# Where the modulation blocks stand: layer 1's move from the MLP product into layer 0's q, k, v and gelu products

## The reference

```python
for l in range(DEPTH):                                   # DEPTH = 2
    mod = (silu(c) @ ada_w[l] + ada_b[l])[:, None, :]    # ada_w[l]: 1024 x 6144
    sh1, sc1, g1, sh2, sc2, g2 = split(mod, 6)
    modc = silu(c_ctx) @ ada_w[l] + ada_b[l]
    h = modulate(rms_norm(x, mix_pre_g[l]), sh1, sc1)    # modulate: h * (1 + scale) + shift
    p = h @ w_in[l]                                      # q, k, v, gelu u, gelu v, conv, gates
    ...
    x = x + g1 * rms_norm(y, mix_post_g[l])
    h2 = modulate(rms_norm(x, ffn_pre_g[l]), sh2, sc2)
    x = x + g2 * rms_norm(square(relu(h2 @ w_ff1[l])) @ w_ff2[l], ffn_post_g[l])
    # the context xc goes the same way with modc, in layer 0
```

## Time and profile before

| | |
|---|---|
| median of 3 runs | 4638.47 us (4631.3 to 4643.43) |
| profiled execution | 4643.45 us, its span 4641.7 us |
| PE busy | 4279.6 us, 92% of the span |
| DVE, ACT, POOL busy | 1254.8, 723.8, 388.0 us |
| mean granted clock of TensorE | 0.954 of full speed |
| chain that ended last | PE 90%, DVE 4%, ACT 4% |

### The profile page before, as it was taken

One profiled execution on the slowest core, in us unless ns is written; L12 is line 12 of the kernel. 1 busy time (PEld: TensorE's weight loads), 2 busy tenths in 40 slices (PEclk: granted clock), 3 DMA queues, 4 the chain that ended last, 5 costly groups with the idle time before them and its releaser, 6 DMA issues.

```text
span 4641.7 us, 34590 instructions
## 1 busy us (share of the span) xinstructions
PE 4279.6 (92%) x13429; PEld 2226.9 (48%) x13429; DVE 1254.8 (27%) x2499; ACT 723.8 (16%) x1393; POOL 388.0 (8%) x250
## 2 busy tenths in 40 slices
PE   7998899997989999997999998989997878699999
PEld 3454555554535445443454443434443467454444
DVE  1213407981010000012341693010003054531010
ACT  2104300002020000002151001110001231231000
POOL 1100002540200000000000132100000001000000
PEclk8999999998999999999999999999998987599999
DMA  5310011111111232221201221222212100101221
GB/s 206 136 55 18 5 55 38 53 55 36 37 68 68 91 127 73 74 72 57 73 19 41 73 73 55 86 84 75 73 68 75 47 19 0 46 29 63 73 78 67
DMA packets 137133, 294.21 MB, mean 63 GB/s; under 512 B 5050, under 2 KB 13290, under 8 KB 137008
## 3 DMA queue, kind: packets, MB, share of 16 engines
q1 hardware_dynamic: 120096, 236.58, 14.5%
q0 software_dynamic: 16912, 55.83, 3.6%
HBM read 290.22 MB, written 2.18 MB: 63 GB/s over the span
## 4 chain that ended last, share of the span: by engine, by line
PE 90%; DVE 4%; ACT 4%; DMA 1%; issue 1%; POOL 0%; DVEq 0%; ACTq 0%; SPq 0%
PE psum L1629 45%; PE psum L1685 14%; PE psum L1891 12%; PE psum L926 5%; PE psum L1623 3%; PE psum L1731 2%; ACT sb_rc L1401 1%; PE psum L1714 1%; PE psum L1671 1%; ACT sb_ht L1401 1%; PE psum L724 1%; DMA sb_ring<-in_ada_w 1%; PE psum L737 1%; PE psum L738 1%; PE psum L1850 0%
## 5 line engine op out<-in xcount | busy, mean ns | idle before, releaser
L1629 PE MATMUL psum<-sb_ht,sb_ring 128*128 128x512 f32 (+1 forms) x4496 | 1664.0, 532 | 16.9 <-ACT sb_rc L1401 8.1
L1629 PEld LDWEIGHTS psum<-sb_ht,sb_ring 128*128 128x128 f32 x4496 | 853.6, 190 | 823.7 <-issue 789.9
L1891 PE MATMUL psum<-sb_ring,sb_rc 128*128 128x512 f32 x1280 | 553.6, 593 | 7.6 <-DVE sb_rc L2142 7.6
L2011 DVE SCALAR_TENSOR_TENSOR sb_rc<-sb_rc,sb_vec x960 | 475.7, 575 | 0.1
L1685 PE MATMUL psum<-sb_ring,sb_ht 128*128 128x512 f32 (+1 forms) x1088 | 458.0, 582 | 2.8 <-ACT sb_ht L1401 2.8
L1891 PEld LDWEIGHTS psum<-sb_ring,sb_rc 128*128 128x128 f32 x1280 | 241.9, 190 | 318.6 <-issue 308.6
L1401 ACT ACTIVATE sb_rc<-psum 128x512 f32 (+3 forms) x238 | 124.9, 545 | 1346.9 <-PE psum L1629 1109.5
L1685 PEld LDWEIGHTS psum<-sb_ring,sb_ht 128*128 128x128 f32 x1088 | 205.9, 190 | 253.3 <-issue 246.8
L1629 PE MATMUL psum<-sb_rc,sb_ring 128*128 128x512 f32 (+1 forms) x768 | 282.0, 529 | 27.6 <-ACT sb_rc L1401 27.6
L1401 ACT ACTIVATE sb_kvt<-psum 128x512 f32<-128x512 f32 (+2 forms) x209 | 105.7, 533 | 1073.1 <-PE psum L1629 852.8
L1623 PE MATMUL psum<-sb_ident,sb_rb 128*128 128x128 f32 (+2 forms) x836 | 135.7, 306 | 142.4 <-DVE sb_rb L1915 37.2
(11 more groups left out here) (288 smaller groups left out, 2741.1 us busy)
## 6 DMA issues: line engine op xcount, KB each, us to landing
sb_ring<-in_w_in SPq DMA_DIRECT2D x37, 2048.0 KB, 7.9
sb_ring<-in_w_ff SPq DMA_DIRECT2D x32, 2048.0 KB, 8.4
sb_ring<-in_w_ffn SPq DMA_DIRECT2D x16, 2048.0 KB, 8.2
sb_kvt<-in_ada_w POOLq DMA_DIRECT2D x12, 2048.0 KB, 9.1
sb_rc<-in_ada_w POOLq DMA_DIRECT2D x8, 2048.0 KB, 8.2
sb_ring<-in_w_out SPq DMA_DIRECT2D x6, 2048.0 KB, 7.8
sb_ring<-in_ada_w SPq DMA_DIRECT2D x4, 2048.0 KB, 12.5
sb_ring<-in_w_gmlp_o SPq DMA_DIRECT2D x4, 2048.0 KB, 7.8
```

Of the source, the lines that this page charges most:

```text
L1629: last = pe.matmul(bank(b + v, m), ring[:, slot, k, j * P:(j + 1) * P], rhs[:, k, a:a + m], start=k == 0, stop=k == KT - 1)
L1891: last = pe.matmul(bank(i), hid[:, KT * kb + k, i * P:(i + 1) * P], ring[:, slot, k, :], start=kb == 0 and k == 0, stop=kb == 1 and k == K ...
L2011: step = stt(conv_slot(j, a, m), conv_slot(j + 1, a + k, m), vec[:, j, k:k + 1], conv_slot(j, a, m), op0=ALU.mult, op1=ALU.add)
```

## The change

All twenty late blocks now stand between groups of layer 0's q, k, v products and gelu u products. Blocks 0 to 11 come after groups 1, 2, 4, 5, 7, 8, 10, 11, 13, 14, 16 and 17 of q, k, v; blocks 12 to 19 after the eight groups of gelu u. The second MLP product has none. All use one weight buffer in `rc`, with the small rows behind it. From block 11 on the results go to banks 6 and 7, before to 0 and 1. Layer 1's blocks' rows are made by DVE inside `normalise_heads`. ACT waits for the last store ahead of the gelu v results, since these overwrite the buffer.

```diff
-        LATE0, LATE = 8, 20
+        LATE0, LATE_B, LATE = 12, 11, 20
...
-        QKV_LATE = [2, 4, 6, 8, 10, 12, 14, 16]
-        order = [(f, c, kb, i) for f in range(2) for c in range(2) for kb in range(2) for i in range(AT)]
-        FF_LATE, FF_LAST = order[2:2 + 3 * (LATE - LATE0):3], order[2 + 3 * (LATE - LATE0)]
+        QKV_LATE = [1, 2, 4, 5, 7, 8, 10, 11, 13, 14, 16, 17]
...
-            if n < LATE0:
-                w, rows, flat = rc[:, RD:RD + KT * COLS], rc, RD - 4 * COLS
-            else:
-                w, rows, flat = kvt[:, 0:KT * COLS], rb, 3 * DM
-            piece = [rows[:, flat + i * COLS:flat + (i + 1) * COLS] for i in range(4)]
+            w = rc[:, RD:RD + KT * COLS]
+            piece = [rc[:, RD + (KT + i) * COLS:RD + (KT + i + 1) * COLS] for i in range(4)]
...
 # PE, late_part(k)
+                if k == LATE_B:
+                    pe.wait_ge(*s_qkv_sb.at(0, 16))
...
 # PE, after the q, k, v products
                 if l == 0:
-                    late_sum(LATE0 - 1)
-                channel_major(s_gu_ps, l, s_gu_sb, 2, 0, ht, l, [s_late_row.at(0, LATE0)] if l == 0 else ())
+                    pe.wait_ge(*s_late_st.at(0, LATE_B))
+                    pe.wait_ge(*s_late_row.at(0, LATE_B))
+                channel_major(s_gu_ps, l, s_gu_sb, 2, 0, ht, l, (),
+                              after=(lambda j: late(LATE0 + j)) if l == 0 else None)
+                if l == 0:
+                    late_sum(LATE - 1)
                 for c in range(2):
-                    token_major(s_gv_ps, l, s_gv_sb, c * n, n, ht, [s_qkv_sb.at(l, 2 * n + AT)] if c == 0 else ())
+                    before = [s_qkv_sb.at(l, 2 * n + AT)] + ([s_late_row.at(0, LATE)] if l == 0 else [])
+                    token_major(s_gv_ps, l, s_gv_sb, c * n, n, ht, () if c else before)
...
 # PE, second MLP product
-                                if l == 0 and (f, c, kb, i) in FF_LATE:
-                                    late(LATE0 + FF_LATE.index((f, c, kb, i)))
-                                if l == 0 and (f, c, kb, i) == FF_LAST:
-                                    late(LATE)
...
 # DVE, normalise_heads, tile u
                     ch.meet()
+                    if l == 0 and u % 2:
+                        late_row(LATE0 - 1 + u // 2)
...
 # ACT, after the q, k, v results
+                drain(s_gu_ps, l, s_gu_sb, lambda j, v, a, m: u_cm[:, j, a:a + m], 0, ACT.Gelu_apprx_tanh,
+                      (lambda j: late_stage(LATE0 + j)) if l == 0 else None)
                 if l == 0:
-                    act.wait_ge(*s_late_out.at(0, 16 * LATE0))
-                drain(s_gu_ps, l, s_gu_sb, lambda j, v, a, m: u_cm[:, j, a:a + m], 0, ACT.Gelu_apprx_tanh)
+                    act.wait_ge(*s_late_out.at(0, 16 * LATE))
```

More of the change, by code:

```diff
@@ L1315, in late_columns @@
             def late_columns(l, parts):
-                pool.wait_ge(*s_late_out.at(0, 16 * (LATE if l else LATE0)))
+                pool.wait_ge(*s_late_out.at(0, 16 * LATE))
                 for part in parts:
@@ L1337, in _ @@
                     late_load(0)
-                    for k in range(1, LATE0):
+                    for k in range(1, LATE):
                         late_load(k)
                         late_store(k - 1)
-                    late_store(LATE0 - 1)
+                    late_store(LATE - 1)
                     late_columns(0, (3, 4))
@@ L1373, in _ @@
                 if l == 0:
[L1374 to L1379, removed]
                     pool.wait_ge(*s_norm_ht.at(1, KT))
@@ L1428, in norm_drain, with drain @@
                     last.then_inc(s_norm_ht.sem, 1)
-            def drain(name, l, out_name, out_of, base, f, streams_=None):
+            def drain(name, l, out_name, out_of, base, f, after=None):
                 for j in range(KT):
                     act.wait_ge(*name.at(l, j + 1))
-                    for v, (a, m) in enumerate(streams_ or streams(l)):
+                    for v, (a, m) in enumerate(streams(l)):
                         last = fn(out_of(j, v, a, m), bank(base + 2 * (j % 2) + v, m), f)
                     last.then_inc(out_name.sem, 1)
+                    if after:
+                        after(j)
             def attention(l):
@@ L1491, in late_stage @@
                     act.wait_ge(*s_late_sum.at(0, k))
-                fn(late_at(k)[1], bank(0 if k < LATE0 else 6)).then_inc(s_late_st.sem, 1)
+                fn(late_at(k)[1], bank(0 if k < LATE_B else 6)).then_inc(s_late_st.sem, 1)
             act.wait_ge(*s_c_in.at(0, 32))
@@ L1631, in product, with channel_major @@
                 return last
-            def channel_major(name, run, used, n, base, rhs, l, before, j0=0):
+            def channel_major(name, run, used, n, base, rhs, l, before, j0=0, after=None):
                 for g in range(j0, j0 + 4 * n):
@@ L1643, in channel_major @@
                     product(base + 2 * (g % 2), slot, g % 4, rhs, streams(l)).then_inc(name.sem, 1)
+                    if after:
+                        after(g)
             def late_part(k):
@@ L1647, in late_part @@
                 pe.wait_ge(*s_late_in.at(0, 32 * (k + 1)))
+                if k == LATE_B:
+                    pe.wait_ge(*s_qkv_sb.at(0, 16))
                 if k:
                     pe.wait_ge(*s_late_st.at(0, k))
-                ada_block(bank(0 if k < LATE0 else 6), w).then_inc(s_late_ps.sem, 1)
+                ada_block(bank(0 if k < LATE_B else 6), w).then_inc(s_late_ps.sem, 1)
             def late_sum(k):
@@ L1655, in late_sum @@
                     pe.wait_ge(*s_late_row.at(0, k))
-                pe.matmul(bank(1 if k < LATE0 else 7)[0:2, :], sel[:, :], late_at(k)[1],
+                pe.matmul(bank(1 if k < LATE_B else 7)[0:2, :], sel[:, :], late_at(k)[1],
                           start=True, stop=True).then_inc(s_late_sum.sem, 1)
             def late(k):
-                if k not in (0, LATE0):
+                if k:
                     late_sum(k - 1)
-                if k < LATE:
-                    late_part(k)
+                late_part(k)
             def ada_block(out_, w):
@@ L2054, in late_row @@
                     dve.wait_ge(*s_late_out.at(0, 16 * k))
-                tt(row, bank(1 if k < LATE0 else 7)[0:2, :], bias, ALU.add).then_inc(s_late_row.sem, 1)
+                tt(row, bank(1 if k < LATE_B else 7)[0:2, :], bias, ALU.add).then_inc(s_late_row.sem, 1)
             def fuse(part, r):
@@ L2094, in _ @@
                         g += 1
-                if l == 0:
-                    late_row(LATE0 - 1)
                 normalise_heads(l)
@@ L2153, in _ @@
                                         post_scale(2 * l + 1, i - 1, rb)
-                                if l == 0 and (f, c, kb, i) in FF_LATE[1:] + [FF_LAST]:
-                                    late_row(LATE0 + (FF_LATE + [FF_LAST]).index((f, c, kb, i)) - 1)
                 post_scale(2 * l + 1, n - 1, rb)
```

4 lines of the change are left out of this document (1 added, 3 removed).

## The result

| | before | after |
|---|---|---|
| median | 4640.36 us (4631.3 to 4645.93, 8 runs) | 4659.06 us (4648.85 to 4659.88, 8 runs) |
| profiled execution, its span | 4643.45 us, 4641.7 us | 4648.85 us, 4647.1 us |
| mean granted clock | 0.954 | 0.956 |

The ratio is 1.0037, with a 95% interval from 1.0026 to 1.0048: 12 to 22 us slower. The time lies inside the predicted range (4636 to 4662), on the predicted side, some 10 us above the 4649.2 that was named and 1 us above the forecast's own range of 4643 to 4658. Six of the eight runs of after lie between 4658.6 and 4659.9, two at 4648.9 and 4649.9, and the profiled one is of these two. So its span says little about the difference, and the stages must be compared one by one.

A forecast was written before the change was run, and what follows sets the result against it. The prediction took PE's (TensorE's) own queue to bound the kernel, its work unchanged and only waits added. Terms of 9.1 + 0.3 + 0.4 + 0.9 = +10.7 us took the median from 4638.47 to 4649.2 us, range 4636 to 4662.

The forecast's parts named there:

- the forecast's own range: Whole kernel: 4643 to 4658 us if the waits come as summed; this case had a chance of 0.60.
- The loads (+9.1 us): q, k, v stage: one weight buffer, so blocks one group apart wait for their load, six times; +9.1 us together.
- Loads beside the ring (the rival at 4657): Blocks after groups 5, 11, 17: loads collide with ring fetches and land later; +18.5 us, 4657; chance 0.12.
- The fourth gelu group (+0.3): Block after the fourth gelu group: its load meets a ring fetch and lands late; +0.3 us, or 0.
- No wait ahead of the gelu products: Start of gelu: the old 1.35 us idle for DVE's row goes, since row 10 is made during block 11.
- Ahead of the gate products (+0.4): After block 19: copy, sum, row and return take 2.73 us against 2.37 ahead of gelu before; net +0.4 us.
- The prediction's own sign of being too low: New profile: idle brackets above 3 us, or idle at other blocks, would make the prediction too low.
- The clock (the rival at 4659.5): q, k, v waits: the clock falls in them, 1.7 us each; in all +21 us, 4659.5; chance 0.08.
- Between the halves (+0.9): Layer 0's second MLP product: without a block between its halves, ACT's copy is no longer hidden; +0.9 us.
- The sum: Whole kernel: the four terms 9.1, 0.3, 0.4 and 0.9 make +10.7 us, bounds 7.5 to 18.5.
- C: Later stages: a theory from the experiments, not the prediction, that they run otherwise because everything is later; no size or chance.
- Faster, the later program falling otherwise: Second block: thin stretches might get clock 1.00, some 16 us less each; two would make 4616; chance 0.07.

The follow-up runs named there:

- e5: Changed kernel plus two row slots, two weight buffers and a mended POOL order (bias row, store, then weights of the block after next): 4644.87 us, ratio 1.0008.
- e4: Kernel before with its own eight q, k, v blocks moved after groups 1, 2, 4, 5, 7, 8, 10, 11, nothing else: 4650.72 us in a single run.
- e1: Changed kernel plus a second slot for the modulation row, so a row waits for the store of two blocks before: 4651.18 us, ratio 1.0018.
- e2: Changed kernel plus two weight buffers for blocks 0 to 11, the order of POOL's queue kept: 4658.65 us, ratio 1.0041.
- e3: Changed kernel plus both the second row slot and the two weight buffers, POOL's order kept: 4653.06 us, ratio 1.0023.
- e8: Kernel before with the blocks of the second MLP product one group earlier, so none stands between its halves: 4640.61 us in a single run.
- e6: e5 plus the last block's sum behind the first gate group, its row and the last store awaited later: 4643.8 us, ratio 1.0002.
- e10: Kernel before plus 12 unused matmuls after the fourth q, k, v group, a delay of 10.3 us: 4649.64 us, ratio 1.0016.
- e7: Kernel before plus 16 unused matmuls after the fourth q, k, v group, a delay of 13.73 us: 4658.27 us, ratio 1.0038.
- e9: Kernel before plus 6 unused matmuls after the fourth q, k, v group, a delay of 5.15 us: 4645.36 us, ratio 1.0010.

## Why the prediction was right, and where it was too low

**The loads (+9.1 us): right, in mechanism and size.** 8.8 us by e5 against after. The waits are at the named places, after groups 2, 5, 8, 11, 14 and 17, and nowhere else; products resume 11.1 to 11.3 us apart as worked out, but 10.88 once and 11.66 for the first pair, which I had taken for the cheapest one: there the bias took 8.5 us to land, not the 7.6 of the earlier trace rows. e4 brings the same waits into the kernel before by distance alone. The load took what the earlier trace rows say: 8.2 to 8.4 us for the weights and 7.6 to 8.5 for the bias in after. The rule of "DMA: Bandwidth & Descriptors" in the Trainium skill (section on the anatomy of one DMA on the gpsimd path) gives an estimate of 6.8 us for the weights; by it they would have been in time, and the trace contradicts it.

**Loads beside the ring (the rival at 4657): wrong,** though its time lies nearer to the measured 4659.06 than the forecast's. The brackets of the three blocks it named are 1.32, 1.17 and 1.21 us, no longer than the others'. The ring's fetch was issued when they had nearly landed (116.01 us, for a block that began at 118.25). What did collide with that fetch is the store issued after it.

**The fourth gelu group (+0.3): 0.** No bracket stands there.

**No wait ahead of the gelu products: right,** and for the reason given. No bracket at 230.79 us: the row that PE waits for is no longer the last one made. e4 bears this out from the other side, since moving the blocks away alone leaves the wait.

**Ahead of the gate products (+0.4): the step that failed.** The prediction summed copy, sum, row and the way back: 2.73 us, 1.7 of it idle. e1 measures just that chain once it is alone, 0.74 + 0.92 = 1.66 us. What it left out is a wait in DVE's own stream: `late_row(k)` asks for the store of row k - 1. In the kernel before two groups or more lay between two rows. Here the last block's sum follows its products directly, so that rows 18 and 19 would stand 3.5 us apart, as they do in e1 (334.15 and 337.63), and the store between them meets the ring's fetch and takes 5.0. It cost 2.65 us more, and the fall of the clock behind it 1.7 us: 4.7 us in place of 0.4. The earlier trace rows had shown that a 4 KB transfer beside a ring fetch lands late; I put that row on the loads and not on the stores. The prediction's own sign of being too low, a bracket above 3 us, is this one of 3.57.

**The clock (the rival at 4659.5): once, and elsewhere.** None of the six waits of 0.94 to 1.72 us brought it down, and e5, without them, had the same busy time for the same 288 records, 126.8 us. So the nearness of its time to the measured one is chance. The longer gap at 337 to 341 us did bring it down once, at the price per fall that the rival had from the earlier trace rows; e2, with the same gap, had the same fall, and e1, e3 and e5, without it, had none. "TensorE: Matmul & The Clock Gate" in the Trainium skill (part on the clock gate) has two levels, 1.2 and 2.4 GHz. The rows agree: 0.50 of full speed from 343 to 345 us, and 1.00 in e1 at the same place.

**Between the halves (+0.9): right,** 0.91 us in after and 0.88 us in e8.

**The sum.** 8.8 + 0 + 4.7 + 0.9 = 14.4 us against 14.1 measured where layer 1 begins, and the interval of the timed runs, 12 to 22 us, holds it. The medians' 18.7 us is more than the chain of causes gives. No cause is shown for the other 4 us, which are within the interval. The prediction drew its line between no change and slower at 13.9 us and gave 0.58 to the one and 0.35 to the other: the medians lie beyond that line, the chain of causes 0.5 us beyond it, and the interval on both sides. That the median still lies inside the range is owed to its upper end, 4662, which was taken from the clock's case, and that did not come as it was forecast.

After's profiled execution loses 5.7 us more on the way from layer 1 to the stage at 3795, from 14.1 to 19.8, though nothing was changed there (windows over this stretch, before first, then after):

```profile
2115.30:3794.70 1679.40, 1537.73 (x4161) 738.29 (x4162) 483.39 (x1014) 278.38 (x496) 130.58 (x69) 0.96 0.18 62
```

```profile
2129.30:3814.30 1685.00, 1542.77 (x4161) 741.24 (x4162) 483.24 (x1014) 278.14 (x496) 129.65 (x69) 0.96 0.18 62
```

The same 4161 records kept PE busy for 5.0 us more. e1, e3, e5, e6 and e10 lose 4.9 to 6.3 us there, e8 3.1, e4 1.1, and e2, e7 and e9 nothing. So it is not bound to the change: e2 has the change and loses nothing, e10 has it not and loses most. But five of the six kernels with the change lose it, and all six have medians 1.6 to 5.0 us further behind before than their row is at layer 1. A single one of these is within its interval; together they leave C open, that the change makes such a loss likelier. No run here decides it.

**Faster, the later program falling otherwise: seen in single executions, in both directions.** The stage of the second block from about 3795 us takes 214 us in before, e2, e3, e4, e7 and e9, 212 in e10, 209 in e1, e5 and e8, and 199 in after and e6 (windows over this stage, before first, then after):

```profile
3795.00:4009.00 214.00, 173.44 (x1344) 152.99 (x1343) 102.74 (x205) 46.32 (x89) 18.27 (x28) 0.74 0.06 20
```

```profile
3814.00:4013.00 199.00, 158.78 (x1342) 143.95 (x1342) 102.64 (x206) 46.08 (x89) 18.24 (x28) 0.82 0.06 20
```

It is the same work, 1342 and 1344 records on PE and the same on DVE and ACT, at a mean granted clock of 0.74 or 0.82, and PE's busy time differs by the 15 us that the stage does. So at this stage the profiled execution of after had a better clock than that of before, worth 15 us, which is how its span comes to be only 5.4 us above that of before while its runs are mostly 10 us slower than it. The two groups of its runs, near 4649 and near 4659, are as far apart as the outcomes of 199 and 209 us of this stage; only the profiled one has a trace here, so that stays open. Whether a later start makes the one or the other outcome likelier is open too.

## What to carry to other kernels

When work is moved closer together, count for each of its resources the distance from its release to its next use: here the weight buffer, whose next user can start 9.4 us after its release (108.84 to 118.25), and a two-row slot, whose store takes 1.6 us alone and 5 us beside a large fetch. A second buffer helps only if nothing in the issuing queue stands ahead of the earlier load (e2 against e5), and the last item of a pipeline, which nothing follows, shows its whole chain unless some other work is put behind it (e6). Where executions of one kernel take different clock outcomes, compare two kernels stage by stage from a common start, and let medians of many runs speak for the end.

## What the runs showed of the hardware

- A store of 4 KB takes 1.6 us by itself and 5.0 to 5.7 us when it is issued 2.0 to 2.7 us behind a fetch of 2 MB on the other queue: five such cases of five in one execution (thirteen of the other fifteen took 1.6, one 2.2 and one 2.9).
- A fall of the granted clock at the start of a dense product cost 1.7 to 1.8 us each time, after idle time of 0.74 + 3.57 us in after and 0.74 + 3.58 in e2, and after thin transposes with 1.4 us idle in e6, e9 and e10, where before, with the same work ahead of it, had none. Waits of 0.9 to 1.7 us with dense products around them never brought it down.
- The same stage of thin products, with the same instructions, took 199, 209, 212 or 214 us in different executions, with mean granted clocks of 0.82, 0.76, 0.75 and 0.74; PE's busy time differed by as much.
